# A two-block transformer layer on one core: a reordered front, a router that picks both experts in all groups at once, and the last pair's usual branch written second

## What is computed

```python
def reference(x, ...):
    x = first_block(x, ...)      # attention (8 window heads, 4 differential heads), then a convolved FFN
    return second_block(x, ...)  # attention (8 dilated, 8 stick-breaking heads), then a routed MoE

# first_block, as far as the change touches it
h = rms_norm(x, attn_pre_g)
proj = einsum("bsd,de->bse", h, w_in)          # q_a 512, k_a 128, v_a 128, q_b 512, k_b 512, v_b 512 columns
lam = exp(sum(lq1 * lk1)) - exp(sum(lq2 * lk2)) + lambda_init

# second_block's router, over 256 tokens: 4 groups of 8 experts
group_prob = softmax(h @ w_group)
group = argmax(group_prob)
exp_logits = (h @ w_expert).reshape(n, 4, 8)[group]
top_p, top_local = top_k(softmax(exp_logits), 2)
top_p = top_p / sum(top_p)
weight = group_gate * top_p
# each of the 32 experts: (silu(xb @ w_gate[e]) * (xb @ w_up[e])) @ w_down[e], 1024x512, 1024x512, 512x1024
```

## Time and profile before

| | |
|---|---|
| time, median of 3 runs | 1000.73 us (1000.51 to 1002.49) |
| the profiled execution | 1001.55 us, of which the span is 999.9 us |
| mean granted TensorE clock | 0.994 |
| PE busy | 973.4 us (97%) |
| DVE, ACT, POOL busy | 550.0, 346.4, 96.6 us |
| read from HBM | 310.47 MB, 312 GB/s over the span |

### The profile page before, as it was taken

One profiled execution on the slowest core, in us unless ns is written; L12 is line 12 of the kernel. 1 busy time (PEld: TensorE's weight loads), 2 busy tenths in 40 slices (PEclk: granted clock), 3 DMA queues, 4 the chain that ended last, 5 costly groups with the idle time before them and its releaser, 6 DMA issues.

```text
span 999.9 us, 15776 instructions
## 1 busy us (share of the span) xinstructions
PE 973.4 (97%) x6129; PEld 672.9 (67%) x6137; DVE 550.0 (55%) x1051; ACT 346.4 (35%) x579; POOL 96.6 (10%) x139
## 2 busy tenths in 40 slices
PE   8999999999999999999999999999999999989896
PEld 6998799999999997989765544445444444433433
DVE  6478689889999998758426322422222222222222
ACT  4665675444454464546332111111111110111102
POOL 8200101011111200200001000600000000000000
PEclk9999999999999999999999999999999999999999
DMA  8424467888789745444938999999999999999995
GB/s 306 170 85 169 153 223 260 290 316 313 285 300 358 275 169 188 148 169 169 391 114 274 380 401 402 417 430 426 427 429 426 427 427 429 428 427 430 430 417 210
DMA packets 61979, 312.21 MB, mean 312 GB/s; under 512 B 4285, under 2 KB 5674, under 8 KB 49130
## 3 DMA queue, kind: packets, MB, share of 16 engines
q1 hardware_dynamic: 54112, 284.83, 71.2%
q0 software_dynamic: 7392, 26.54, 7.5%
q10 hardware_dynamic: 426, 0.16, 0.1%
HBM read 310.47 MB, written 1.05 MB: 312 GB/s over the span
## 4 chain that ended last, share of the span: by engine, by line
PE 77%; DMA 11%; DVE 7%; issue 2%; ACT 2%; POOL 0%; SPq 0%; DVEq 0%; ACTq 0%
PE bank L972 10%; PE bank L1538 10%; PE bank L974 10%; PE bank L973 10%; PE bank L1557 10%; PE bank L1592 8%; DMA eslots<-in_w_gate 8%; PE bank L1459 4%; PE bank L1119 3%; DVE ring_r L2049 2%; PE bank L1469 2%; DMA ring<-in_w_in 2%; PE bank L1047 1%; DMA ring<-in_w_up 1%; PE bank L1085 1%
## 5 line engine op out<-in xcount | busy, mean ns | idle before, releaser
L972 PE MATMUL bank<-hT_r,ring_r 128*128 128x256 f32 x664 | 189.4, 285 | 1.4 <-DVE ring_r L2049 1.3
L974 PE MATMUL bank<-hT_r,ring_r 128*128 128x256 f32 x664 | 187.9, 283 | 0.0
L2049 DVE TENSOR_TENSOR ring_r<-ring,ring_r 128x2048 fp32r<-128x2048 f32 (+1 forms) x74 | 164.6, 2258 | 13.9 <-ACT ring_r L1677 13.6
L1677 ACT ACTIVATE ring_r<-ring 128x2048 fp32r<-128x2048 f32 (+1 forms) x74 | 136.5, 1890 | 42.6 <-DMA ring<-in_w_up 34.6
L973 PE MATMUL bank<-v_tok_r,ring_r 128*128 128x256 f32 x496 | 140.4, 283 | 0.0
L972 PEld LDWEIGHTS bank<-hT_r,ring_r 128*128 128x128 f32 x664 | 127.4, 192 | 2.4 <-DVE ring_r L2049 1.6
L974 PEld LDWEIGHTS bank<-hT_r,ring_r 128*128 128x128 f32 x664 | 127.4, 192 | 0.0
L1592 PE MATMUL bank<-eslots,scratch 128*64 128x512 f32 x496 | 113.4, 595 | 0.7 <-ACT scratch L1929 0.7
L973 PEld LDWEIGHTS bank<-v_tok_r,ring_r 128*128 128x128 f32 x496 | 95.2, 192 | 0.2
L974 PE MATMUL bank<-ring_r,hn_r 128*128 128x512 f32 (+2 forms) x220 | 80.4, 365 | 0.0
L1592 PEld LDWEIGHTS bank<-eslots,scratch 128*64 128x64 f32 x496 | 35.7, 137 | 62.9 <-issue 61.0
(11 more groups left out here) (359 smaller groups left out, 1598.7 us busy)
## 6 DMA issues: line engine op xcount, KB each, us to landing
eslots<-in_w_gate SPq DMA_DIRECT2D x28, 2048.0 KB, 23.7
eslots<-in_w_up SPq DMA_DIRECT2D x28, 2048.0 KB, 23.5
eslots<-in_w_down SPq DMA_DIRECT2D x27, 2048.0 KB, 27.1
ring<-in_w_up SPq DMA_DIRECT2D x16, 2048.0 KB, 11.8
ring<-in_w_in SPq DMA_DIRECT2D x9, 2048.0 KB, 7.9
ring<-in_w_down SPq DMA_DIRECT2D x8, 2048.0 KB, 9.0
kT<-in_w_ada POOLq DMA_DIRECT2D x24, 512.0 KB, 7.6
ring<-in_w_out SPq DMA_DIRECT2D x4, 2048.0 KB, 9.0
```

What stands on the lines that cost most here:

```text
L972: pe.matmul(dst, lhs[0], rhs[0], start=start, stop=False, **flags)
L974: return pe.matmul(dst, lhs[1], rhs[0], start=False, stop=stop, **flags)
L1677: sc.activation(hi, raw, ACT.Copy).then_inc(s_whi, 1)
L2049: last = ve.tensor_tensor(lo, raw, hi, ALU.subtract)
```

## The change

- **Front, loads**: the first chunk's half 0 is loaded, rounded and subtracted in two quarters of 0.5 MB with semaphores of their own. Twelve of the small loads go from ACT's queue to SP's, between chunks 1 and 2.
- **Front, PE**: the 6 zeros ahead of tile 0 go, the 3 ahead of tile 1 become 1. Items 0 to 3 start on quarters. Item 4 runs its products with rounded weights before it waits for the rest of the chunk. Item 5 makes the values turned (`vT`, 24 matmuls of 256 columns), DVE takes them to PT, and a new item 7 (`turn`) turns them back with two transposes; the later items move by one, and so change between ACT and DVE.
- **Front, ACT and DVE**: ACT takes items 0 and 2 before it splits chunk 2. DVE's lambda goes behind the splits of chunk 2. In DVE's attention loop the splits stand before the takes.
- **Router**: ACT makes the second copy of `lgT`. Both experts are found in all four groups at once on 64-wide operands (both token tiles in one instruction), and masked by the group afterwards. iota begins at 1, so that `rank1` and `slots(0)` are one instruction. The last residual product, and `s_acc` with it, goes behind the ranks. Of PE's products of zeros, the one ahead of the wait for `s_A` is dropped, and the 4 between ranks and dispatch become 1.
- **Last pair**: the two `If`s of PE change places.

```diff
-        items1 += [(1, "ka", (0, 0)), (1, "v", (P, P, 0))]
+        items1 += [(1, "ka", (0, 0)), (1, "vT", (P, 0))]
-        items1 += [q_item(0), k_item(0), q_item(1), ...
+        items1 += [q_item(0), (1, "turn", (0, 0)), k_item(0), q_item(1), ...
-        BETWEEN = [{0: [7], 1: [8], 2: [9], ...
+        BETWEEN = [{0: [7, 8], 1: [9], 2: [10], ...
...
+            if kind == "vT":
+                return [(PT[:, 0, 0:S], bank[:, 0:S])]
+            if kind == "turn":
+                return [(vt[:, :, 0:P], bank[:, 0:S].rearrange("p (t n) -> p t n", t=T))]
...
-            for half, done in enumerate((s_loaded_once, loaded[0])):
-                tiles_of_half = slice(half * KD // 2, (half + 1) * KD // 2)
-                sp.dma_start(raw[:, tiles_of_half, :], w_in[:, tiles_of_half, 0:HALF]).then_inc(done, 16)
-            for c in range(1, LANES):
-                straight(N_IN + c, w_in[:, :, c * HALF:(c + 1) * HALF])
+            for first, end, done in ((0, 2, s_loaded_once), (2, 4, loaded[SLOT_N + 3]), (4, KD, loaded[0])):
+                sp.dma_start(raw[:, first:end, :], w_in[:, first:end, 0:HALF]).then_inc(done, 16)
+            straight(N_IN + 1, w_in[:, :, HALF:2 * HALF])
+            sp.dma_start(stage[:, 0, :], cw[0:P, :]).then_inc(s_stage, 16)
...
+            straight(N_IN + 2, w_in[:, :, 2 * HALF:3 * HALF])
...
+                if kind == "turn":
+                    piece_taken(blk, AHEAD[0])
+                    for t in range(T):
+                        last = pe.transpose(bank[:, t * P:(t + 1) * P], PT[:, 0, t * P:(t + 1) * P], ident[:, :])
...
-            stay_awake(PS[7], 6)
             turn("attn1", hn, range(T - 1))
-            stay_awake(PS[6], 3)
+            stay_awake(PS[6], 1)
             turn("attn1", hn, range(T - 1, T))
...
+            def project_rounded_first(n):
...
+                pe.wait_ge(s_whi, 2 * (N_IN + c) + 2)
+                for k in range(KD):
+                    for part in range(2):
+                        pe.matmul(dst, w[0][:, k, c0:c0 + P], tiles("attn1", k)[part], ...
+                split_ready(N_IN + c)
...
-            for b in range(2 * T):
+            for b in range(2 * T - 1):
+                residual(b)
...
             last.then_inc(s_rank, 1)
+            residual(2 * T - 1).then_inc(s_acc, 1)
...
-            stay_awake(PS[4], 1)
             pe.wait_ge(s_A, 1)
...
-            stay_awake(PS[4], 4)
+            stay_awake(PS[4], 1)
             dispatch(0)
...
-            with pe.If(n_pairs < PAIRS + 1):
-                pair(PAIRS - 1, PAIRS - 1, last_one=True)
-                combine_last(PAIRS - 1)
             with pe.If(n_pairs > PAIRS):
...
+            with pe.If(n_pairs < PAIRS + 1):
+                pair(PAIRS - 1, PAIRS - 1, last_one=True)
+                combine_last(PAIRS - 1)
...
-            split_one(N_IN, 0)
+            for quarter, (done, ready) in enumerate(((s_loaded_once, s_whi_first), (loaded[SLOT_N + 3], s_whi))):
+                sc.wait_ge(done, 16)
+                raw, hi, _ = first_quarter(quarter)
+                sc.activation(hi, raw, ACT.Copy).then_inc(ready, 1)
...
             split(N_IN + 1)
+            take(0, range(4))
             split(N_IN + 2)
...
-                    take(blk, fill.get(i, []))
                     for half_of_chunk in splits.get(i - 1, ()):
                         split_one(*half_of_chunk)
+                    take(blk, fill.get(i, []))
...
+            ve.tensor_reduce(gmax, groups, X, ALU.max)
+            then(ve.tensor_reduce(m1, experts, X, ALU.max))
+            for t in range(T):
+                ve.scalar_tensor_tensor(gfirst[:, t, :], ..., ALU.is_lt, ALU.add)
+            then(ve.tensor_tensor(by_group(first), experts, in_group(m1), ALU.is_lt))
+            ve.tensor_reduce(gidx, gfirst, X, ALU.min)
+            then(ve.tensor_tensor(first, first, both_tiles(frac), ALU.add))
+            ve.tensor_scalar(ngmax, gmax, -1.0, None, ALU.mult).then_inc(s_r1, 1)
+            then(ve.tensor_reduce(i1, by_group(first), X, ALU.min))
             for t in range(T):
+                ve.tensor_scalar(inside[:, t, :], frac[:, 0:NGRP], gidx[:, t:t + 1], None, ALU.is_equal)
+            then(ve.tensor_tensor(by_group(A1), by_group(both_tiles(frac)), in_group(i1), ALU.is_equal))
+            then(ve.scalar_tensor_tensor(by_group(el2), by_group(A1), 2 * NEG, experts, ALU.mult, ALU.add))
+            ve.tensor_tensor(by_group(A1), by_group(A1), in_group(inside), ALU.mult)
+            then(ve.tensor_reduce(m2, by_group(el2), X, ALU.max))
+            ve.scalar_tensor_tensor(by_group(places_in), in_group(inside), -1.0, ..., ALU.mult, ALU.add)
+            then(ve.tensor_tensor(by_group(first), by_group(el2), in_group(m2), ALU.is_lt))
+            ve.tensor_tensor(m2, m2, m1, ALU.subtract)
+            then(ve.tensor_tensor(first, first, places_in, ALU.add))
+            then(ve.tensor_reduce(i2, by_group(first), X, ALU.min))
+            then(ve.scalar_tensor_tensor(by_group(A2), ..., in_group(i2), ALU.add, ALU.is_equal))
             ve.tensor_tensor(Aa, A1, A2, ALU.add).then_inc(s_A, 1)
+            then(ve.tensor_tensor(m2, m2, inside, ALU.mult))
+            ve.tensor_reduce(ed, m2, X, ALU.add).then_inc(s_r1, 1)
```

More of the change, by code:

```diff
@@ L595, in needs @@
                 return AHEAD[0]
-            return (15 if values else 10) if i < 9 else (16 if values else 14)
+            return (16 if values else 11) if i < 9 else (17 if values else 15)
         def turned(u):
@@ L1222, in project_first @@
                     last.then_inc(s_gemm[0], 1)
+            def project_rounded_first(n):
+                c, kind, (c0, _) = items1[n]
+                assert kind == "ka" and n < AHEAD[0]
+                w = split_view((N_IN + c) % LANES)
+                dst = item_bank(0, n)[:, 0:S]
+                pe.wait_ge(s_whi, 2 * (N_IN + c) + 2)
+                for k in range(KD):
+                    for part in range(2):
+                        pe.matmul(dst, w[0][:, k, c0:c0 + P], tiles("attn1", k)[part],
+                                  start=(k == 0 and part == 0), stop=False)
+                split_ready(N_IN + c)
+                for k in range(KD):
+                    last = pe.matmul(dst, w[1][:, k, c0:c0 + P], tiles("attn1", k)[0], start=False,
+                                     stop=(k == KD - 1))
+                last.then_inc(s_gemm[0], 1)
             pe.wait_ge(s_vec, 1)
@@ L1226, in _ @@
             turn_gains()
-            for n in range(4, AHEAD[0] + 1):
+            project_rounded_first(4)
+            for n in range(5, AHEAD[0] + 1):
                 if n == AHEAD[0]:
@@ L1671, in split_one @@
             def split_one(n, part, more=0):
[L1672 to L1674 removed]
+                if n == N_IN or part == 0:
                     sc.wait_ge(loaded[n % LANES], 16 * (n // LANES + 1) + 16 * more)
@@ L1787, in _ @@
             sc.activation(lam2, lam2, ACT.Exp).then_inc(s_lame, 1)
-            take(0, range(AHEAD[0] + 1))
+            take(0, range(4, AHEAD[0] + 1))
             sc.wait_ge(s_vec, 2)
@@ L2470, in over_n, with by_group, in_group, both_tiles @@
                 return v.unsqueeze(2).broadcast_to([P, T, n])
-            experts = lambda v, t: v[:, t, :].rearrange("p (g j) -> p g j", j=EPG)
-            def first_largest(v, largest, dst):
-                for t in range(T):
-                    last = ve.scalar_tensor_tensor(dst[:, t, :], v[:, t, :], largest[:, t:t + 1], frac[:, 0:v.shape[2]],
-                                                   ALU.is_lt, ALU.add)
-                then(last)
-            def one_hot(dst, at):
-                for t in range(T):
-                    last = ve.tensor_scalar(dst[:, t, :], frac, at[:, t:t + 1], None, ALU.is_equal)
-                return last
+            def by_group(v):
+                return v.rearrange("p t (g j) -> p t g j", j=EPG)
+            def in_group(v):
+                return v.unsqueeze(3).broadcast_to([P, T, NGRP, EPG])
+            def both_tiles(v):
+                return v.unsqueeze(1).broadcast_to([P, T, v.shape[1]])
             ve.wait_ge(s_lg, 1)
-            for half in range(2):
-                last = ve.tensor_copy(lgT[half], PS[4][64 * half:64 * half + NL, 0:S])
-            last.then_inc(s_lgT, 1)
+            ve.tensor_copy(lgT[0], PS[4][0:NL, 0:S]).then_inc(s_lgT, 1)
             ve.wait_ge(s_wshift, 2)
@@ L2506, in _ @@
-            then(last)
-            for t in range(T):
-                last = ve.tensor_tensor(experts(el, t), lg[:, t, NGRP:].rearrange("p (g j) -> p g j", j=EPG),
-                                        outside[:, t, :].unsqueeze(2).broadcast_to([P, NGRP, EPG]), ALU.add)
-            then(last)
-            then(ve.tensor_reduce(m1, el, X, ALU.max))
-            first_largest(el, m1, first)
-            then(ve.tensor_reduce(i1, first, X, ALU.min))
-            then(one_hot(A1, i1))
-            then(ve.scalar_tensor_tensor(el2, A1, 2 * NEG, el, ALU.mult, ALU.add))
@@ L2606, in pair @@
```

(1 more changed line is left out.)

104 lines of the change are left out of this document (56 added, 48 removed).

## The result

The changed kernel takes 1012.13 us (median of 4, 1011.01 to 1014.95) against 1001.53 us (median of 4) of the kernel before on the same chip: a ratio of 1.0107, 95% interval 1.0093 to 1.0122. It is slower by about 10.7 us. The forecast was 996.6, within 994.3 to 999.0. The profiled execution has a span of 1010.8 us against 999.9.

What follows compares the result with a forecast made beforehand. PE, busy 973.4 of 999.9 us, was taken as the bound, with the experts' weight stream as full. Front -4.3, router -0.8, last pair +1.0 gave -4.1: 997.4 from 1001.55, less 0.82, 996.6 us; range 994.3 to 999.0.

Steps and rivals of the forecast that it cites:

- the term of the last pair: Swapped Ifs at the last pair: a jump of 3.69 us leaves PE standing still, +1.0 us.
- rival D: Last pair's jump must fetch through full DMA queues; at 10.5 us the time is 1003.4; chance 0.03.
- The front: Start to first scores: earlier first product -2.1, lighter items -2.5, transposes +0.3, together -4.3 us.
- The lighter items: Items 4 and 5 of the front: a wait hidden and fewer, wider matmuls, taken as 2.5 us saved.
- The cover of 0.5 us: Front: DVE finishes chunk 2's rest at 32.6, first scores end at 33.1, so PE need not wait.
- the forecast transposes: Item 7, behind the first scores: two transposes of the values on PE, costing 0.3 us.
- rival A: Front gives less: w_in lands no earlier (1.2 us) and k0 waits for DVE (0.8); 998.6, chance 0.20.
- The router: Router: DVE's chain shrinks from 15 dependent steps to 12, taken as -0.8 us.
- Rival E: Router: the chain of broad operands is as long as the old one; 997.4, chance 0.08.
- rival B: Front: with most zeros gone the first products run at half clock, costing 1.7 us; 998.3, chance 0.07.
- the stream moves with PE: Experts: moving PE ahead of 620 us moves weight stream and end equally; gate waits stay near 7.0 us.
- three times the even share and the 0.87: Front: upper bound of the gain at the first product, put at 3.0 us.

Runs made afterwards that it cites:

- e2: The changed kernel with the two Ifs of PE in the old order and no padding; ratio 0.9989 to the kernel before.
- e11: The changed kernel with 60 never-executed instructions in the body that is jumped over, no padding ahead of the loop; ratio 1.0016 to the kernel before.
- e1: The changed kernel with 60 padding instructions on PE ahead of the loop, swapped Ifs kept; ratio 0.9985 to the kernel before.
- e9: The kernel before with the two Ifs of PE swapped and nothing else; ratio 1.0026 to the kernel before.
- e4: The kernel before with 150 padding instructions added on PE ahead of the loop; ratio 1.0031 to the kernel before.
- e3: The changed kernel with 60 padding instructions on PE ahead of the loop and the Ifs in the old order; ratio 0.9972 to the kernel before.
- e8: e3 with the four lambda loads moved from SP's queue to ACT's; ratio 1.0012 to the kernel before.
- e6: e3 with 35 padding instructions ahead of the loop in place of 60; 998.02 us in a single run.
- e7: e3 with the twelve small loads moved back from SP's queue to ACT's; ratio 0.9960 to the kernel before.
- e12: e3 with DVE's lambda inputs behind takes and splits, and ACT's exponential behind the takes; ratio 0.9959 to the kernel before.
- e10: e1 with 196 never-executed instructions in the body that is jumped over; ratio 1.0054 to the kernel before.

## Why the prediction was wrong

**The step that failed** is the term of the last pair, +1.0 us, together with what all terms assumed: that the place of the other code stays as it is. The term priced the swap as one slow jump, with one stop of PE. Measured at the place where the change had put the code, the swap costs 11.8 us (the changed kernel over e2). Of these 9.1 us are gone when 60 instructions that never run move the jump's target (e11). Each edit was costed by the instructions that it issues, and nothing was put down for where the code behind it comes to lie.

**The loop's jump** was priced at nothing for the same reason. The prediction said of it only, against rival D, that its jumps had taken 83 and 217 ns "under the same stream", "though they may have had their code at hand". They had it at hand by a margin that a removal of about 60 instructions used up: the jump back takes 5.9 to 6.1 us in the kernels with these edits, which costs 1.7 to 3.1 us, the lower value not clear of noise. This is not in the sum, and it is in no rival.

**The last pair** in detail. The forecast took the old jump's 3.69 us, and 1.0 us of standing still. The jump took 5.96 to 6.19 us in every kernel that had it, with a stop of 2.99 to 3.17 us; in the old order it took 3.3 to 4.0 us in all profiles, at 987 to 995 us. That the full weight stream makes the difference, as rival D has it, fits, but place and stream changed together and no run parts them. The forecast's way from the jump to the stop was right: 5.96 - 3.1 + 0.4 = 3.3 us for 2.99. The half clock behind it was left out: 3.4 us of it in e1 and e11 (none in e9), though the earlier trace rows showed such a stretch behind a wait. And a jump can stop PE twice: the target's block comes, and if the target lies near its end, the next one must be fetched too, another 3.91 to 4.47 us. Rival D had the right place, with the point at which it decides at 7.8 us for a single jump; the jump alone never came near it. Its chance of 0.03 was too low for what two stops cost.

**The front**, forecast -4.3. At the first product -1.80 for -2.1, and -1.0 to -1.6 in the other profiles with these edits. The 12.22 that all this is counted from was itself late: e4 and e9, which have the old front, start at 11.88 and 11.90. From mean to mean (12.00 of three, 10.85 of nine) the gain is 1.15, so the lower end of 0.9 was nearer. The lighter items gave 2.61 for 2.5: with no wait the first scores stand 22.48 - 1.49 = 20.99 us behind the first product, for 23.60. The cover of 0.5 us, called thin, was not there: the sum had DVE at its takes at about 25.8, and they began at 28.25. What was missed is that a load moved into SP's queue moves the later loads of that queue, the lambda vectors among them; the prediction looked at chunk 2 alone. Of the 2.92 us at the scores 2.40 are left at the router (542.30 for 544.70): 0.5 went between, of which 0.3 would be the forecast transposes. To the gate products -3.1 for -5.1, as rival A had it; on the time, -2.8 (e3).

**The router** was right. The first reduction and the release of DVE's chain in the kernel after:

```profile
544.74 0.16 DVE L2536 TENSOR_REDUCE scratch<-scratch 128x2 f32<-128x8 f32 x1
...
548.68 0.23 DVE L2560 TENSOR_TENSOR scratch<-scratch 128x64 f32<-128x64 f32 x1
```

These are 548.68 + 0.23 - 544.74 = 4.17 us for the 4.92 of the earlier trace rows, and from the product at 542.30 to the ranks at 548.97 are 6.67 us, for 7.41 before: a gain of 0.74 against the forecast 0.8. Rival E falls. Behind the ranks, where nothing was to change, the first gate product follows after 5.73 us against 5.72.

**The clock in the front** (rival B) did not fall, though 8 of 9 zeros are gone; the stretch of the kernel after:

```profile
0.00:36.00 36.00, 31.78 (x227) 27.30 (x228) 25.21 (x43) 19.66 (x27) 27.13 (x34) 1.00 0.84 300
```

The granted clock is 1.00 throughout, and it is so ahead of the experts in every other profile with these edits but e8's. The 12 first zeros, the turns and the one zero left were enough there. The rule on transposes in the Trainium skill ("TensorE: Matmul & The Clock Gate", section "Part 4: PE-mode transpose") had let one fear otherwise; no run has the turns alone, so it isn't tested. e8 shows that the fear had ground: when the first product came at 13.48, the stretch behind it was at half clock, as rival B has it. The prediction saw such a stretch once in the kernel before. There are two of 3.4 us, the other from 879.7 to 883.1, both near a wait of PE for gate weights.

**That the stream moves with PE** holds in part. The gate waits stay near 7 us where the loop stays (7.7 in e3, 7.2 in e6, 7.5 in e7, 7.0 before), but with the waits for up and down weights these three wait 9.3 to 9.5 us for weights in all, and e12 8.4. So 1.4 to 2.5 us of what was gained ahead of the experts went into waits for weights in these profiled executions. In the changed kernel, where PE itself is late, 2.7 us of its stops are taken from these waits.

One bound of the sum was off: three times the even share and the 0.87 are 2.7, not 3.0. It changes nothing in the result.

The span then adds up: -3.1 at the first gate product, +12.2 in stops for "issue", -2.7 in waits for weights, and for the clock: PE is busy for 2.7 + 5.2 + 6.2 = 14.1 us at half clock, which costs 7.1, against 6.8 / 2 = 3.4 for the two stretches before; +3.7. Together +10.1 of the 10.9.

## What to carry to other kernels

In a kernel like this one, with a loop of 1636 instructions in PE's instruction memory of 2048 (the size is that of the Trainium skill, as above), every instruction added or removed ahead of the loop is an edit of the loop too: compare the count of instruction packets and the durations of the taken branches before and after, before you read anything else, and if a change that takes code away is slower, try it with padding. A taken jump out of the fetched code took here 6 us on the sequencer and stopped PE for 3, and it cost another 6.9 us of time if its target lay just ahead of a block's end (e10 over e1), so the usual way should fall through. A load that is moved into a queue delays whatever follows it in that queue: look for the first reader of each.

## What was not expected of the hardware

- Instructions that never run changed the time by 6.9 us (e10 over e1) and by -9.1 us (e11 against the changed kernel).
- A loop of 1636 instructions ran its second pass without a fetch when padded by 35 and by 60 instructions, and was fetched whole when padded by 0 and by 20.
- Like stops of PE were followed by half clock in one kernel and not in another. Behind its stop of 3.05 us at the last pair e1 ran 3.4 us at 1.2 GHz; e9 stopped there for 3.10 us and stayed at 2.4 GHz. The two stops of the changed kernel there, 2.99 and 3.91, had 10.2 us at 1.2 GHz.
